# Moving the attention projection between gate units, and the decode rows' loads to GpSimd's queue, in a float32 hybrid decoder layer

## The reference, cut to what matters

```python
h = rmsnorm(x, g_mp)
q, k, v, u, vs, ga, gb = split(h @ w_in)          # ga, gb: 1024 columns each
o_a, rows = core(q, k, v)                         # prompt: dilated windows; decode rows: 129 keys of a cache
vs = layernorm(gelu(vs)); o_b = gelu(u) * spatial_mix(vs)
m = sigmoid(ga) * (o_a @ w_pa) + sigmoid(gb) * (o_b @ w_pb)
x = x + rmsnorm(m @ w_o, g_mq)
h = rmsnorm(x, g_fp)
x = x + rmsnorm((silu(h @ w_g) * (h @ w_u)) @ w_d, g_fq)
```

## Time and profile before

| | |
|---|---|
| median of 3 runs | 1645.75 us |
| the profiled execution, its own time | 1645.16 us |
| its span in the profile | 1643.4 us |
| mean granted TensorE clock | 0.995 |
| busy: PE, DVE, ACT, POOL | 1563.9, 559.4, 483.7, 134.3 us |

### The profile page before, as it was taken

One profiled execution on the slowest core, in us unless ns is written; L12 is line 12 of the kernel. 1 busy time (PEld: TensorE's weight loads), 2 busy tenths in 40 slices (PEclk: granted clock), 3 DMA queues, 4 the chain that ended last, 5 costly groups with the idle time before them and its releaser, 6 DMA issues.

```text
span 1643.4 us, 23725 instructions
## 1 busy us (share of the span) xinstructions
PE 1563.9 (95%) x9929; PEld 1506.7 (92%) x9929; DVE 559.4 (34%) x1037; ACT 483.7 (29%) x915; POOL 134.3 (8%) x125
## 2 busy tenths in 40 slices
PE   5999999999999999988999999999999999999995
PEld 4999999889998898866878999999999999999995
DVE  7104550343014444164563232122123113212336
ACT  5215543432223312133765211211121121111123
POOL 6000000000000000041001000100110010010014
PEclk9999999999999999999999999999999999999998
DMA  5111112000102016142331211111111111111102
GB/s 193 39 51 39 39 57 76 26 27 27 52 27 81 27 50 183 34 155 90 116 115 35 81 52 50 42 52 40 52 49 43 52 39 52 40 52 52 39 26 104
DMA packets 132534, 100.81 MB, mean 61 GB/s; under 512 B 4872, under 2 KB 121360, under 8 KB 132432
## 3 DMA queue, kind: packets, MB, share of 16 engines
q1 hardware_dynamic: 126912, 94.06, 18.3%
q10 hardware_dynamic: 5520, 5.25, 1.0%
HBM read 91.56 MB, written 7.73 MB: 60 GB/s over the span
## 4 chain that ended last, share of the span: by engine, by line
PE 86%; DVE 6%; ACT 2%; DMA 2%; issue 2%; POOL 1%; ACTq 0%; POOLq 0%; DVEq 0%
PE bank L878 29%; PE bank L474 10%; PE bank L476 9%; PE bank L475 9%; PE bank L886 5%; PE bank L888 5%; PE bank L887 5%; PE psT L470 3%; DMA qb<-q_rows 2%; PE psC L658 1%; PE psA L658 1%; PE bank L846 1%; PE bank L847 1%; PE bank L848 1%; DVE pr L1574 1%
## 5 line engine op out<-in xcount | busy, mean ns | idle before, releaser
L878 PE MATMUL bank<-f_hi,w_hi 128*128 128x384 f32 (+1 forms) x1056 | 339.1, 321 | 6.4 <-issue 3.8
L1464 DVE TENSOR_TENSOR w_lo<-w_raw,w_hi 128x1024 fp32r<-128x1024 f32 x138 | 171.4, 1243 | 495.6 <-ACT w_hi L1391 231.3
L474 PE MATMUL bank<-h_hi,w_hi 128*128 128x344 f32 x1008 | 334.9, 332 | 3.8 <-DVE w_lo L1464 2.3
L878 PE MATMUL bank<-f_hi,w_lo 128*128 128x384 f32 (+1 forms) x1056 | 337.7, 320 | 0.0
L878 PE MATMUL bank<-f_lo,w_hi 128*128 128x384 f32 (+1 forms) x1056 | 337.4, 319 | 0.0
L476 PE MATMUL bank<-h_hi,w_lo 128*128 128x344 f32 x1008 | 322.7, 320 | 0.0
L475 PE MATMUL bank<-h_lo,w_hi 128*128 128x344 f32 x1008 | 322.5, 320 | 0.0
L878 PEld LDWEIGHTS bank<-f_hi,w_hi 128*128 128x128 f32 x1056 | 198.5, 188 | 8.2 <-issue 4.4
L474 PEld LDWEIGHTS bank<-h_hi,w_hi 128*128 128x128 f32 x1008 | 190.7, 189 | 9.2 <-issue 3.9
L878 PEld LDWEIGHTS bank<-f_lo,w_hi 128*128 128x128 f32 x1056 | 198.5, 188 | 0.0
L878 PEld LDWEIGHTS bank<-f_hi,w_lo 128*128 128x128 f32 x1056 | 198.4, 188 | 0.0
(11 more groups left out here) (390 smaller groups left out, 1865.6 us busy)
## 6 DMA issues: line engine op xcount, KB each, us to landing
w_raw<-in_w_in SPq DMA_DIRECT2D x42, 512.0 KB, 4.0
w_raw<-in_w_out SPq DMA_DIRECT2D x24, 512.0 KB, 3.6
w_raw<-in_w_gate SPq DMA_DIRECT2D x23, 512.0 KB, 3.9
w_raw<-in_w_up SPq DMA_DIRECT2D x23, 512.0 KB, 3.9
w_raw<-in_w_down SPq DMA_DIRECT2D x22, 512.0 KB, 3.4
xin<-in_x_prompt SPq DMA_DIRECT2D x8, 512.0 KB, 7.6
xn<-in_x_prompt SPq DMA_DIRECT2D x8, 512.0 KB, 6.6
out_y_prompt<-xn SPq DMA_DIRECT2D x8, 512.0 KB
```

The source lines that it names most:

```text
L474: mm(out[:, 0:TG], w_hi[par][:, ws], hi[:, k, tgc[tg]], start=first, stop=False)
L878: ins = mm(out[:, 0:NG[tg]], w[par][:, ws], x[tg][:, k, :], start=(k == 0 and w is w_hi and x is f_hi), stop=(k == KD - 1 and w is w_lo))
L1464: v.tensor_tensor(w_lo[par][:], w_raw[par][:], w_hi[par][:].bitcast(F32), ALU.subtract).then_inc(w_lo_s, 1)
```

## The change

- The gate units are cut in two stages: `ga` with j = 0 to 5, then `pa`, then `gc` with j = 6 and 7. SP loads the weights in that order.
- The decode steps move ahead: self scores to (3, 1), score rows to (4, 0), probabilities turned to (4, 1), and the 27 slots to (4, 2) to (5, 2) (`PV_AT`).
- The store of `q_rows`, the 48 loads of keys and queries, and the 24 loads of values are issued by POOL, in this order and before its first `m_lo`. Keys and queries have 4 buffers each. DVE scores eight pairs per unit.
- The merge works in place: `pt` is gone, products and totals are written over `ga` (chunks 0 to 5) or `p67` (chunks 6 and 7, to which ACT copies the projection's bank); for those two chunks the product is made when the gate's tanh is there. Totals trail the products by half.
- `xn` is reloaded three tiles at a time among the `wo` loads. `m_lo` and `y2` change places with `f_lo` (regions 3 and 4).

```diff
-          ("ga", 8, 8), ("pa", 2, 8), ("wo", 24, 0), ("ffn", 62, 80), ("tail", 6, 12)]
+          ("ga", 6, 6), ("pa", 2, 8), ("gc", 2, 2), ("wo", 24, 0), ("ffn", 62, 80), ("tail", 6, 12)]
@@ SP
+            for i in range(6):
+                load_ga(U0["ga"] + i, i)
+            sp.wait_ge(s_nc, 5)
 ...
+            for i in range(2):
+                load_ga(U0["gc"] + i, 6 + i)
 ...
+                for n in range(8):
+                    u = U0["wo"] + 8 * g + n
+                    load_w(u, u % 2, chunks(A["w_out"][0], 256 * (n % 4), 2, 512 * (n // 4), 512), 2)
+                    t = 3 * g + n - 2
+                    if 2 <= n < 5 and t < 8:
+                        if t == 0:
+                            sp.wait_ge(full[2], M0["wo"])
+                        sp.dma_start(xn[:, t, :], xp[t]).then_inc(xr_in[t], 16)
@@ PE
+            PV_AT = {(4, 2): (3, 0, 5), (5, 0): (0, 5, 13), (5, 1): (0, 13, 21), (5, 2): (0, 21, 27)}
 ...
+            for j in range(2):
+                u = U0["gc"] + j
+                unit(u, M0["gc"] + j, u % 2, 8, h_hi, h_lo)
@@ ACT
-                    if 2 <= 3 * j + tg < 14:
-                        load_k(2 * (3 * j + tg) - 4)
-                        load_k(2 * (3 * j + tg) - 3)
 ...
+                split_in(U0["ga"], 0, 0, j, M0["ga"] + j + 1)
+                if j == 4:
+                    oa_high(0)
+                    oa_high(1)
             act.wait_ge(s_oa, 2)
             oa_high(2)
 ...
+            for k in range(18, 24):
+                pa_copy(k)
+                m_high(k - 10)
+            split_in(U0["pa"], 0, 0, 1, M0["pa"] + 8)
 ...
+            for k in range(18, 24):
+                j, tg = k // 3 - 6, k % 3
+                act.wait_ge(full[tg], M0["gc"] + j + 1)
+                if k >= 20:
+                    act.wait_ge(ga_s, k - 19)
+                fn(gt[:, k % 2, :], bank[tg][:, 0:TG], ACT.Tanh, scale=0.5).then_inc(free[tg], 1)
+                if tg == 2:
+                    split_in(U0["gc"], 0, 0, j, M0["gc"] + j + 1)
+                m_high(k)
@@ DVE
-            for j in range(8):
-                for kk in range(max(6 * j - 6, 0), min(6 * j, 24)):
+            for j in range(6):
+                for kk in range(max(8 * j - 8, 0), min(8 * j, 24)):
                     if kk == 2:
                         merge_sum(1)
                     k_scores(kk)
 ...
+            for k in range(18):
+                merge_product(k)
+                if k % 2:
+                    merge_total(k // 2)
+                if k == 15:
+                    lo_in(U0["pa"], 0, 0, 0)
+            for k in range(9, 18):
+                merge_total(k)
+                if k == 14:
+                    lo_in(U0["pa"], 0, 0, 1)
+            for k in range(18, 24):
+                merge_product(k)
+                merge_total(k)
+                if k % 3 == 2:
+                    lo_in(U0["gc"], 0, 0, k // 3 - 6)
@@ POOL
+            pool.wait_ge(s_nc, 5)
+            pool.dma_start(q_rows, qtok[:].rearrange("b g c -> b (g c)")).then_inc(q_out, 16)
+            pool.wait_ge(q_out, 16)
+            for kk in range(24):
+                (rows, ck), n, g = cache(kk), kk // 3, kk % 3
+                if kk >= 4:
+                    pool.wait_ge(s_kq, kk - 3)
+                pool.dma_start(kraw[0:ck, kk % 4, :], rows[:, 0, :]).then_inc(sk_in[kk % 4], 16)
+                pool.dma_start(qb[0:ck, kk % 4, :], q_rows[n:n + 1, 256 * g:256 * g + 256].broadcast_to([ck, 256])
+                               ).then_inc(sq_in[kk % 4], 16)
+            pool.wait_ge(mg_done, 4)
+            pool.wait_ge(at_gu, 26)
+            for kk in range(24):
+                rows, ck = cache(kk)
+                pool.dma_start(cv[0:ck, kk, :], rows[:, 1, :]).then_inc(sv_in, 16)
```

More of the change, by code:

```diff
@@ L192, in build @@
         VTO = _o + 256
-        ga, _ = at("ga", [P, KD, NT], F32, R4)
-        f_lo = [at(f"f_lo{g}", [P, KD, NG[g]], F32R, R4 + 4 * KD * RG[g])[0] for g in range(3)]
+        ga, _o = at("ga", [P, 6, NT], F32, R4)
+        oa_hi, _ = at("oa_hi", [P, 2, NT], F32R, _o)
+        kraw, _o = at("kraw", [P, 4, 256], F32, _o)
+        qb, _o = at("qb", [P, 4, 256], F32, _o)
+        assert _o <= X
+        f_lo = [at(f"f_lo{g}", [P, KD, NG[g]], F32R, R[3] + 4 * KD * RG[g])[0] for g in range(3)]
         xin = [at(f"xin{i}", [P, D], F32, R4 + 4096 * i)[0] for i in range(8)]
@@ L280, in build @@
         q_out = sem("s_query_stored")
[L281 removed]
+        sk_in, sq_in = [[sem(f"{name}{i}") for i in range(4)] for name in ("k_cache_landed", "s_query_landed")]
         sv_in = sem("v_cache_landed")
@@ L389, in _, with load_ga @@
                     store_kv(1)
-            for i in range(8):
-                u = U0["ga"] + i
+            def load_ga(u, i):
                 load_w(u, u % 2, chunks(w_in, 0, 8, GA_COL + P * i, P), 8)
[L394 to L403, removed]
+            for i in range(6):
+                load_ga(U0["ga"] + i, i)
+            sp.wait_ge(s_nc, 5)
             for g in range(GROUPS):
@@ L808, in sample_pv @@
                         ins.then_inc(s_pv, 1)
+            PV_AT = {(4, 2): (3, 0, 5), (5, 0): (0, 5, 13), (5, 1): (0, 13, 21), (5, 2): (0, 21, 27)}
             def pv_aside(j, tg):
-                first = 24 * (j - 6) + 8 * tg - 12
-                return {k: (lambda c=first + k: sample_pv(c)) for k in range(8) if 0 <= first + k < 27} if j >= 6 else None
-            for j in range(8):
+                if (j, tg) not in PV_AT:
+                    return None
+                k0, c0, c1 = PV_AT[j, tg]
+                return {k0 + c - c0: (lambda c=c: sample_pv(c)) for c in range(c0, c1)}
+            for j in range(6):
                 u = U0["ga"] + j
@@ L1201, in oa_high @@
             def oa_high(tg):
-                act.wait_ge(full[tg], M0["pa"])
                 act.wait_ge(mg_done, 4)
+                act.wait_ge(s_kq, 24)
                 fn(oa_hi[:, :, tgc[tg]], oaT[:, :, tgc[tg]], ACT.Copy).then_inc(oa_h, 1)
             act.wait_ge(kv_d, 16 * 52)
[L1208 to L1220, removed]
+            for j in range(6):
                 for tg in range(3):
@@ L1228, in _, with m_part, m_high, pa_copy @@
                     merge_in(1, j, tg)
-                    if 2 <= 3 * j + tg < 14:
-                        load_k(2 * (3 * j + tg) - 4)
-                        load_k(2 * (3 * j + tg) - 3)
[L1232 to L1235, removed]
+                split_in(U0["ga"], 0, 0, j, M0["ga"] + j + 1)
+                if j == 4:
+                    oa_high(0)
+                    oa_high(1)
             act.wait_ge(s_oa, 2)
             oa_high(2)
-            split_in(U0["ga"], 0, 0, 7, M0["ga"] + 8)
-            for k in range(24):
+            def m_part(k):
+                return (ga[:, k // 3] if k < 18 else p67[:, k // 3 - 6])[:, tgc[k % 3]]
+            def m_high(k):
                 act.wait_ge(m_t, k + 1)
-                fn(m_hi[:, k // 3, tgc[k % 3]], pt[:, 2 * (k % 2) + 1, :], ACT.Copy).then_inc(m_h, 1)
-                if k % 12 == 11:
-                    split_in(U0["pa"], 0, 0, k // 12, M0["pa"] + 4 * (k // 12) + 4)
+                fn(m_hi[:, k // 3, tgc[k % 3]], m_part(k), ACT.Copy).then_inc(m_h, 1)
+            def pa_copy(k):
+                act.wait_ge(full[k % 3], M0["pa"] + k // 3 + 1)
+                fn(m_part(k), bank[k % 3][:, 0:TG], ACT.Copy).then_inc(free[k % 3], 1)
+            for k in range(5):
+                m_high(k)
+            split_in(U0["pa"], 0, 0, 0, M0["pa"] + 4)
+            for k in range(5, 8):
+                m_high(k)
+            for k in range(18, 24):
+                pa_copy(k)
+                m_high(k - 10)
+            split_in(U0["pa"], 0, 0, 1, M0["pa"] + 8)
+            for k in range(14, 18):
+                m_high(k)
+            for k in range(18, 24):
[6 more added lines that the diff above has]
+                    split_in(U0["gc"], 0, 0, j, M0["gc"] + j + 1)
+                m_high(k)
             def split_out(w):
@@ L1734, in _ @@
                     v.tensor_copy(spT[0:NS, 3:6, :].rearrange("p g n -> p (g n)"), psA[0:NS, 96:192]).then_inc(s_ptc, 1)
-                if j == 7:
+                if j == 5:
                     oa_low(0)
-                else:
-                    lo_in(U0["ga"], 0, 0, j)
+                    oa_low(1)
+                lo_in(U0["ga"], 0, 0, j)
             dve.wait_ge(s_pv, 1)
@@ L1743, in _, with m_part @@
                               ).then_inc(s_oa, 1)
-            oa_low(1)
             oa_low(2)
-            lo_in(U0["ga"], 0, 0, 7)
+            def m_part(k):
+                return (ga[:, k // 3] if k < 18 else p67[:, k // 3 - 6])[:, tgc[k % 3]]
             def merge_product(k):
[L1751 to L1769, removed]
+                if k < 18:
+                    dve.wait_ge(full[k % 3], M0["pa"] + k // 3 + 1)
+                    v.scalar_tensor_tensor(m_part(k), m_part(k), 1.0, bank[k % 3][:, 0:TG], ALU.add, ALU.mult
```

(12 more changed lines are left out.)

51 lines of the change are left out of this document (21 added, 30 removed).

## The result

The changed kernel takes 1632.86 us (median of 12 executions) against 1646.16 us for the kernel before on the same chip: a ratio of 0.9934, 95% interval 0.9911 to 0.9956. It is faster by 0.7%; the prediction of 1652 us had the wrong sign. The executions of a kernel here fall into two groups 17 to 22 us apart, the upper one at a mean clock of about 0.98 instead of 0.99 (4 of 12 for the changed kernel, 11 of 61 for the one before over the whole study), and within the lower group the medians are 1632.4 us against 1646.1. Where I add or subtract microseconds I compare profiled executions, part by part.

A forecast was written before the change was run, and what follows sets the result against it. PE was busy 95% of the span, so only its idle time and low clock could be won. Terms: -27.9 + 5.0, about -23, then +28.5 + 1.8, gives +7.3 us on 1645.2: 1652 us, range 1620 to 1672.

The forecast's parts named there:

- the price of an issue by GpSimd: Decode transfers on POOL's queue: 73 issues one after the other at r us each, r taken as 1.0.
- 60r - 31.5: PE's wait at the first value slots for the load stream, r us per issue: 28.5 us at r = 1.0.
- -23: Sum in us with loads that arrive in time: 27.9 removed from `ga` to the fourth `wo` unit, 5.0 added.
- cheap issue: Rival: POOL issues like ACT, 0.45 to 0.6 us each; 1622 to 1628 us; chance 0.19.
- halfway: Rival: an issue takes 0.6 to 0.82 us, part of the gain survives; 1634 us at 0.7; chance 0.22.
- `pa` at PE's rate: `pa` stage: in-place products and totals remove all 13.9 us lost, leaving about 23 us behind its first wait.
- The last six jobs by ACT copies: In `gc`, ACT copies and runs `m_high` in turn, about 0.95 us a job against PE's 0.94: cost 0, at most 1.
- `wo` without its 0.9 + 3.5 + 1.8 us: First `wo` units: the loss at the start, the second unit's `w_lo` wait and the low clock all go.
- New wait before `pa` 3.2 us and low clock 1.8: `pa` begins right behind the decode output: PE waits 3.2 us and a low clock follows, cost 5.0 us.
- The scores in time if loads are cheap: Gate units: the 3.0 us wait for decode scores and 1.8 us of low clock go if scores are in time.
- POOL's waits cost nothing: Waits added to POOL: only more loads, then `m_lo`, stand behind them, and POOL was idle 127.98 us there; cost 0.
- A low clock of 1.8 us after each wait: PE: a wait of 3.0 to 3.5 us was each time followed by a low clock worth 1.8 us.

The follow-up runs named there:

- the first experiment: Changed kernel with the decode step's 73 transfers issued on SP's queue instead of GpSimd's: median 1645.05 us, ratio 0.9933.
- the reordering: Changed kernel with `oa_hi` and `oa_lo` of the last third ahead of the second `pa` unit's split and `lo_in`: 1630.21 us, ratio 0.9912.
- twice the issues: Changed kernel with each of the 72 loads split into two of half the partitions, 145 transfers on GpSimd's queue: 1672.21 us, ratio 1.0151.
- both orders: Changed kernel with `oa_hi`, `oa_lo` before the second `pa` unit's split, `lo_in`, and the `sst` copy before the fourth gate unit's `lo_in`: 1647.68 us.
- the values on GpSimd: Kernel before with only the 24 value loads issued by GpSimd instead of SP: two executions, 1668.9 and 1670.0 us.
- the best kernel: Changed kernel with both orders and the decode step's 73 transfers on SP's queue: 1619.64 us, ratio 0.9821; run again 1621.08 us, ratio 0.9816.

## Why the prediction was wrong, step by step

**The step that failed** is the price of an issue by GpSimd. The prediction took r = 1.0 us, by scaling ACT's 0.45 with POOL's slowness in arithmetic. It measured 0.54. The term 60r - 31.5 is then 0.9 us and not 28.5, and that alone turns the sign: -23 + 0.9 + 1.8 gives about 1625 us, inside the rival called cheap issue. The row that was the same operation was the nearer one, even from another engine; the factor of two between POOL and DVE was measured on arithmetic and did not carry over. The longest of the 72 load issues took 0.59 us, so nothing on DVE lengthened them either. With loads of r = 1.03 PE waited for the stream where the formula put it, 22.2 us against its 30.3. So the mechanism stood and this size was wrong.

With the right r the sum is still 7.6 us below the measured 1632.5. Three terms make that up but for 0.3 us: the tail, 4.4 us, which the prediction put at nothing, the wait at the scores with its low clock, 4.6 us instead of the 2.7 above, and 1.0 us by which `ga` begins later. That the measured time lies near the rival called halfway (1634) is luck: its r of 0.6 to 0.82 was not what GpSimd took.

In the Trainium skill, the page Perfetto Trace Analysis (DMA Instruction — SWDGE (GPSIMD)) says that such a row ends when the last of GpSimd's processors has made its descriptors, not when data has moved. The trace agrees: the row ends after 0.54 us, and the data lands 3.1 us (`kraw`) or 2.6 us (`cv`) after the issue. In the Trainium skill, the page DMA: Bandwidth & Descriptors (Latency and other measured facts) gives about 1 us to the first byte against 0.6 us for the hardware path. That is a latency, and I weighed it as an occupancy. No gap of 0.4 us shows in the landing times of the 128 KB loads: from POOL 3.1, 3.4 and 2.6 us (`kraw`, `qb`, `cv`), from SP in the first experiment 2.9, 3.7 and 2.3.

**The rest,** in the prediction's order:
- `pa` at PE's rate: right. 27.31 us are 22.6 of work, 2.9 of wait and 1.8 of low clock. In-place writing alone gives 6.1 of the 13.9 us, since DVE then binds at 1.17 us a job. The prediction had DVE's 1.84 us per two jobs for one total, which is the changed kernel; it named the half rate only for `m_lo`.
- The last six jobs by ACT copies: right, `gc` took 22.64 us with no wait. `wo` without its 0.9 + 3.5 + 1.8 us: right, 16.71 us. The `xn` loads at 0: right, no wait in `wo`.
- New wait before `pa` 3.2 us and low clock 1.8: right, 2.9 and 1.7 to 1.8, and the reordering shows that it is the order of the operations behind the last tanh. The wait was not wholly new: in the kernel before 1.2 us of it were there, inside the 13.9.
- The scores in time if loads are cheap (3.0 + 1.8 us gone): wrong. Keys and queries ran at 0.68 us per issue (616.17 to 640.81 us for 36), not at 0.54, because POOL stood 5.7 us in six waits for DVE to free one of four buffers. (The 18.1 us of the row above hold 12.4 from before that.) The last product came at 642.43, a `lo_in` of 1.20 us stood ahead of the copy, and PE waited 2.9 us. This and its low clock of 1.7 us are 4.6 us.
- POOL's waits cost nothing: right for the `m_lo` that stand behind them. Not foreseen was the tail, 4.4 us. The profiled execution's account closes with these: 1645.2 - 23 = 1622.2, and 4.6, 4.4 and 1.0 for the later start of `ga` make 1632.2 (measured 1632.5).
- A low clock of 1.8 us after each wait: right in this profiled execution. What it leaves out is the long stretch, worth about 23 us by the traces.

**What stays open.** Why the tail is longer: it was 2.1 to 2.3 us with 0, 1 or 24 transfers on GpSimd's queue, 4.3 with 49, 6.6 with 73, and 5.3 with 145 of half the rows. It goes with that queue, since moving the loads to SP took it away both times, but not in step with a count. The row that puts it down to PE names an engine that had long been done.

And what sets off a long low stretch. It is not the length of the wait: behind 6.2 us the lower clock was over after 10 us, behind 1.7 us came the long one. What the four traces with a long stretch have in common is its place. It began 3.1 to 4.3 us after the first of the 27 slots (at 652.5 us with the loads on SP, 667.7 with twice the issues, 653.0 with both orders, 680.2 with the values on GpSimd), covered the rest of them, and ended 3.6 to 4.9 us after the last one. In the traces of the kernel before, the changed and the best kernel, the slots ran at the upper level. So the small matmuls of the slots, of two columns each, are a rival to the wait as the cause, or a part of it, and no kernel was run that has one without the other. That the waits matter is argued from counts: 7 of 10 and 9 of 10 executions lay in the upper group with waits of 1.3 to 1.7 us and none of 10 without such a wait. But with waits of 2.4 to 3.0 us it was only 2 of 10, 4 of 12, 3 of 10 and 11 of 61, and with 6.2 us none of 4. That the upper group is the long stretch was seen in the traces of the loads on SP, of both orders and of the values on GpSimd; for the others it is inferred from their mean clock of 0.98.

## What to carry to other kernels

Price an operation by rows of the same operation before scaling by another kind of work on the same engine: a DMA issue is not arithmetic. When one edit takes away a buffer wait, compute what each engine then needs per job, with all of its operations; here in-place writing moved the bound from POOL to DVE, whose totals are slower beside POOL's work, and PE ran free only in the kernel that also halved the totals' rate. And a wait of PE of 1 to 3 us can be dearer than its own length: look at the granted clock behind it, as far as the next stage of small matmuls. Putting the one operation that PE waits for ahead of those that it doesn't, with the loads on SP's queue, took the kernel from 1646 to 1620 us.

## What the runs showed of the hardware

- GpSimd issued a plain load every 0.5 to 0.6 us, for 128 and 32 rows of 1 KB (changed kernel) and for 64 and 16 rows (kernel with halves: 48 in 24.64 us) alike; SP's issues had medians of 0.43 us for the same loads (first experiment).
- TensorE stood at its lower clock (1.2 GHz) for 47 us with PE busy all the time (178 matmuls where 300 fit at the upper level of 2.4 GHz). In all four traces that have such a stretch it covers the slots with matmuls of two columns.
- A DVE total (two inputs of 128x344, float32) took 0.50 to 0.52 us with POOL still and 0.80 to 0.83 us while POOL wrote `m_lo` throughout (in place alone).
- With 49 and more transfers on GpSimd's queue the program ended 2.2 to 4.5 us later after its last store than with 24 or fewer.
